# Grouped-query attention: reciprocal softmax sums spread over partitions through a row in DRAM instead of by products with the identity

## The reference, cut to what matters

```
q, k = rms_norm(q, q_norm_w), rms_norm(k, k_norm_w)
q, k = apply_rope(q, cos, sin), apply_rope(k, cos, sin)
p = softmax(einsum("bhgqd,bhkd->bhgqk", q, k) * 64 ** -0.5)
o = einsum("bhgqk,bhkd->bhgqd", p, v)
return o @ w_o
```

## Time and profile before

| what | value |
| --- | --- |
| time, median of 3 runs | 3609.38 us (3599.21 to 3609.42) |
| time of the profiled execution | 3618.67 us |
| span of the profiled execution, first to last instruction | 3616.9 us |
| TensorE busy | 3342.2 us, 92% of the span |
| VectorE busy | 1868.7 us, 52% |
| ScalarE busy | 1185.8 us, 33% |
| GpSimd busy | 942.6 us, 26% |
| mean granted TensorE clock | 0.964 of full |
| DMA, mean over the span | 64 GB/s |

### The profile page before, as it was taken

One profiled execution on the slowest core, in us unless ns is written; L12 is line 12 of the kernel. 1 busy time (PEld: TensorE's weight loads), 2 busy tenths in 40 slices (PEclk: granted clock), 3 DMA queues, 4 the chain that ended last, 5 costly groups with the idle time before them and its releaser, 6 DMA issues. The chain is left out here.

```text
span 3616.9 us, 51583 instructions
## 1 busy us (share of the span) xinstructions
PE 3342.2 (92%) x20797; PEld 3084.3 (85%) x20797; DVE 1868.7 (52%) x2655; ACT 1185.8 (33%) x2106; POOL 942.6 (26%) x726
## 2 busy tenths in 40 slices
PE   5898898998889999999988999999798999999997
PEld 4777777887789999999988777777598999999996
DVE  4555555555155554555545555565416545555454
ACT  3334344444232222122223555555413121222111
POOL 1122112222233322223233121221133322332221
PEclk8999999998899999999999999999899999999998
DMA  6333343113211111111112111101231111111101
GB/s 240 108 107 113 112 125 116 51 40 121 87 42 47 41 53 35 41 37 39 54 38 78 38 30 26 35 23 35 97 99 58 42 36 41 41 37 56 35 29 59
DMA packets 206659, 229.78 MB, mean 64 GB/s; under 512 B 30564, under 2 KB 173533, under 8 KB 205341
## 3 DMA queue, kind: packets, MB, share of 16 engines
q1 hardware_dynamic: 186973, 162.69, 14.8%
q10 hardware_dynamic: 11664, 42.47, 3.5%
q0 software_dynamic: 7856, 22.29, 1.7%
HBM read 181.79 MB, written 31.98 MB: 59 GB/s over the span
## 5 line engine op out<-in xcount | busy, mean ns | idle before, releaser
L205 PE MATMUL psum<-Hh,wh 128*128 128x384 f32 x3360 | 1142.2, 340 | 52.6 <-ACT Hh L377 14.7
L206 PE MATMUL psum<-Hh,wl 128*128 128x384 f32 x3360 | 1131.0, 337 | 0.0
L207 PE MATMUL psum<-Hl,wh 128*128 128x384 f32 x3360 | 1130.9, 337 | 0.0
L286 DVE SCALAR_TENSOR_TENSOR x<-psum,mod,x 128x384 f32<-128x384 f32 (+2 forms) x768 | 377.4, 514 | 684.6 <-PE psum L207 643.2
L205 PEld LDWEIGHTS psum<-Hh,wh 128*128 128x128 f32 x3360 | 636.6, 189 | 63.3 <-issue 35.5
L206 PEld LDWEIGHTS psum<-Hh,wl 128*128 128x128 f32 x3360 | 636.8, 190 | 0.0
L207 PEld LDWEIGHTS psum<-Hl,wh 128*128 128x128 f32 x3360 | 636.5, 189 | 0.0
L816 POOL TENSOR_TENSOR wl<-wr,wh 128x1024 fp32r<-128x1024 f32 x88 | 219.8, 2498 | 986.6 <-ACT wh L735 986.6
L766 ACT ACTIVATE ff_u<-psum 128x768 f32<-128x768 f32 x88 | 71.6, 814 | 1109.2 <-PE psum L207 1109.2
L205 PE MATMUL psum<-ff_ah,ff_dh 128*128 128x384 f32 x1056 | 365.1, 346 | 29.4 <-POOL ff_al L838 20.7
L964 DVE SCALAR_TENSOR_TENSOR ff_c<-ff_u,par,ff_c 128x1153 f32<-128x1153 f32 x176 | 377.4, 2144 | 15.8 <-DVE ff_c L961 5.2
(11 more groups left out here) (217 smaller groups left out, 4267.8 us busy)
## 6 DMA issues: line engine op xcount, KB each, us to landing
wr<-w_up SPq DMA_DIRECT2D x88, 512.0 KB, 3.9
ff_dr<-w_down SPq DMA_DIRECT2D x22, 1024.0 KB, 6.1
da_mw<-mod_w ACTq DMA_DIRECT2D x40, 512.0 KB, 3.9
wr<-mod_w ACTq DMA_DIRECT2D x40, 512.0 KB, 4.8
wr<-w_qkv_diff SPq DMA_DIRECT2D x24, 512.0 KB, 19.2
x<-x_save SPq DMA_DIRECT2D x16, 576.0 KB, 7.5
in_mw<-mod_w SPq DMA_DIRECT2D x8, 1024.0 KB, 12.2
Hh<-oh_save SPq DMA_DIRECT2D x14, 576.0 KB, 9.8
```

The lines of the kernel that those rows point to most:

```text
L205: pe.matmul(out, w_hi, m_hi, start=start, stop=False)
L206: pe.matmul(out, w_lo, m_hi, start=False, stop=False)
L207: return pe.matmul(out, w_hi, m_lo, start=False, stop=stop)
L286: last = dve.scalar_tensor_tensor(g.x[:, m, lo:hi], g.PS[:, bank, lo - n * NB:hi - n * NB], g.mod[:, gate + m, cond:cond + 1], g.x[:, m, l ...
```

## The change

For each pair, the reciprocals no longer go through TensorE. DVE writes `rl` with the two heads outermost. SP's new `spread_sums` waits for them, sends them to a small row buffer in DRAM (`rl_rows`, 512 numbers of 4 bytes, one by one), waits for that to land, and reads them back with two DMAs, each of which puts one head's row of up to 256 numbers on 64 partitions of `rb`. ACT copies half a bank, DVE multiplies `yb` by `rb`. The division of pair 4 moves from step 0 of the next head (where it stood behind nothing but its wait) to step 1, behind that step's maxima. In SP's program the swap of head j+1 comes behind `spread_sums(j, 0)`; `spread_sums(j, 1)` to `(j, 4)` come behind the swap and ahead of the next head's weight load; the first output weights come between `spread_sums(7, 0)` and `(7, 1)`; and the wait for head 6's stores and `load_outputs`, unchanged in the text, now stand behind `spread_sums(7, 4)`. TensorE's first wait for the reciprocals goes; each third block of the value product also waits for the copy of head m = 0's group.

```
--- before.py
+++ after.py
@@ -152,6 +152,7 @@
         g.lam = sb("lam", [P, 4])
         g.Hh = sb("Hh", [P, KC, T], F32R)
         g.Hl = sb("Hl", [P, KC, T], F32R)
+        g.rl_rows = nc.dram_tensor("rl_rows", [2, 2, 2, P], F32, kind="Internal").ap()
         g.x_save = nc.dram_tensor("x_save", [P, KC, T], F32, kind="Internal").ap()
         g.wr = sb("wr", [P, 2, KC, P])
         g.wh = sb("wh", [P, 2, KC, P], F32R)
@@ -1832,17 +1833,13 @@
         "cos": ([P, NS], F32), "sin": ([P, NS], F32), "q": ([P, T], F32), "rot": ([P, NS], F32), "sq": ([P, T], F32),
         "nqh": ([P, 2, T], F32R), "nql": ([P, 2, T], F32R), "nkh": ([P, 2, KW], F32R), "nkl": ([P, 2, KW], F32R),
         "v": ([P, 2, KW // P, P], F32), "e": ([P, 2, NKEY], F32), "pt": ([P, 2, TT, 2 * P], F32),
-        "yb": ([P, 2, 2 * P], F32), "y": ([P, 2, 2 * P], F32), "yh": ([P, 2 * P], F32R), "yl": ([P, 2 * P], F32R),
+        "yb": ([P, 2 * P], F32), "rb": ([P, 2, 2 * P], F32), "y": ([P, 2, 2 * P], F32), "yh": ([P, 2 * P], F32R), "yl": ([P, 2 * P], F32R),
         "nm": ([P, 2], F32), "nb": ([P, 2], F32), "l": ([P, 4, 2], F32), "rl": ([P, 2, 2], F32), "wq": ([P, 1], F32),
         "ms": ([P, TT, 2], F32), "rk": ([P, 2, TT, 2], F32), "r": ([P, 2, TT, 2], F32)},
         "tab w_in0 w_in1 w_hi w_lo free0 free1 full free2 free3 free4 ahead side sq_d ck_in ck_d cv_in ko_d v_st k_st ms_d r_d normed kswap swap rope"
-        " s_mm mx nmax exp rl_d pv_out y_d y_split y_out wq_d wo_in0 wo_in1 wo_hi wo_lo o_in")
+        " s_mm mx nmax exp rl_d rl_out rl_in pv_out y_d y_split y_out wq_d wo_in0 wo_in1 wo_hi wo_lo o_in")
     free = {"F": b.free0, "C": b.free1, 0: b.free2, 1: b.free3, 2: b.free4}
     w_in = [b.w_in0, b.w_in1]
-    BC0 = 2 * P
-
-
-
     early = b.pt[:, :, :, :].rearrange("p m c q -> p (m c q)")
     k = [early[:, p * KW:(p + 1) * KW] for p in range(2)]
     vt = [early[:, 2 * KW:2 * KW + T], early[:, 0:T]]
@@ -1906,6 +1903,22 @@
                 ring.wait_read(sp, free, ("vt", p, 2))
                 for m in range(2):
                     sp.dma_start(a.new_v_gqa[0, 0, 2 * p + m], b.v[:, p, KW // P - 1, m * DH:(m + 1) * DH]).then_inc(b.v_st, 16)
+
+            def spread_sums(j, p):
+
+                n, done = PAIRS[p][1], len(PAIRS) * j + p
+                sp.wait_ge(b.rl_d, done + 1)
+                if done >= 2:
+                    sp.wait_ge(b.rl_in, 32 * (done - 1))
+                rows = g.rl_rows[done % 2]
+                sp.dma_start(rows.rearrange("m i q -> q (m i)"), b.rl[:, :, :].rearrange("p m i -> p (m i)"),
+                             allow_slow_non_contiguous=True).then_inc(b.rl_out, 16)
+                if done >= 2:
+                    sp.wait_ge(b.y_d, done - 1)
+                sp.wait_ge(b.rl_out, 16 * done + 16)
+                for m in range(2):
+                    sp.dma_start(b.rb[m * DH:(m + 1) * DH, done % 2, 0:n * P],
+                                 rows[m, 0:n].rearrange("i q -> (i q)").partition_broadcast(DH)).then_inc(b.rl_in, 16)
 
             load_w(("K", 1))
             load_w(("V", 0))
@@ -1930,11 +1943,15 @@
             for j in range(HEADS):
                 if j + 3 < HEADS:
                     load_w(("Q", j + 3))
+                spread_sums(j, 0)
                 if j + 1 < HEADS:
                     swap_queries(j + 1)
-            sp.wait_ge(b.w_lo, len(UNITS) - 2)
-            sp.wait_ge(b.full, ring.done(("Q", HEADS - 1, NN - 1)))
-            first_out_weights(g, sp, b, 1)
+                for p in range(1, len(PAIRS)):
+                    if (j, p) == (HEADS - 1, 1):
+                        sp.wait_ge(b.w_lo, len(UNITS) - 2)
+                        sp.wait_ge(b.full, ring.done(("Q", HEADS - 1, NN - 1)))
+                        first_out_weights(g, sp, b, 1)
+                    spread_sums(j, p)
             sp.wait_ge(b.y_out, 32 * len(PAIRS) * (HEADS - 1) + 16)
             load_outputs(g, sp, b)
             sp.wait_ge(b.o_in, OUT_LOADS)
@@ -2013,8 +2030,7 @@
                     act.wait_ge(b.full, ring.done(use))
                     if done:
                         act.wait_ge(b.y_d, done)
-                    act.activation(b.yb[:, :, 0:n], ring.bank(g, use).rearrange("p (a t) -> p a t", a=2)[:, :, 0:n],
-                                   ACT.Copy).then_inc(free[ring.place[use]], 1)
+                    act.activation(b.yb[:, 0:n], ring.bank(g, use)[:, 0:n], ACT.Copy).then_inc(free[ring.place[use]], 1)
 
             act.wait_ge(b.wq_d, 1)
             for n in range(2):
@@ -2185,16 +2201,12 @@
                 use, (t0, n) = ("PV", j, p), PAIRS[p]
                 out = ring.bank(g, use)
                 ring.wait_free(pe, free, use)
-                pe.wait_ge(b.rl_d, len(PAIRS) * j + p + 1)
-                for i in range(n):
-                    broadcast_heads(g, pe, out[:, BC0 + i * P:BC0 + (i + 1) * P], b.rl[:, i, :])
                 if p == 0 and j % 4 == 0:
                     pe.wait_ge(b.cv_in, 16 * 4)
                 t, nk = t0 + n - 1, keys(t0) // P
                 for c in range(nk):
-                    if nk == 1:
-                        ring.wait_read(pe, free, ("T", j, t, 0, 0))
                     if c % 3 == 0:
+                        ring.wait_read(pe, free, ("T", j, t, 0, c // 3))
                         ring.wait_read(pe, free, ("T", j, t, 1, c // 3))
                     for m in range(2):
                         last = pe.matmul(out[m * DH:(m + 1) * DH, 0:n * P], b.v[:, j // 4, value_chunk(t0, c), m * DH:(m + 1) * DH],
@@ -2299,14 +2311,17 @@
             def sums(j, p):
                 t0, n = PAIRS[p]
                 dve.wait_ge(b.exp, 2 * (TILES * j + t0 + n))
-                dve.reciprocal(b.rl[:, 0:n, :], b.l[:, t0 % 4:t0 % 4 + n, :]).then_inc(b.rl_d, 1)
+                if j or p:
+                    dve.wait_ge(b.rl_out, 16 * (len(PAIRS) * j + p))
+                dve.reciprocal(b.rl[:, :, 0:n], b.l[:, t0 % 4:t0 % 4 + n, :].rearrange("p i m -> p m i")).then_inc(b.rl_d, 1)
 
             def divide(j, p):
                 n, done = PAIRS[p][1] * P, len(PAIRS) * j + p
                 ring.wait_read(dve, free, ("PV", j, p))
+                dve.wait_ge(b.rl_in, 32 * (done + 1))
                 if done >= 2:
                     dve.wait_ge(b.y_split, 2 * (done - 1))
-                dve.tensor_tensor(b.y[:, done % 2, 0:n], b.yb[:, 0, 0:n], b.yb[:, 1, 0:n], ALU.mult).then_inc(b.y_d, 1)
+                dve.tensor_tensor(b.y[:, done % 2, 0:n], b.yb[:, 0:n], b.rb[:, done % 2, 0:n], ALU.mult).then_inc(b.y_d, 1)
 
             dve.tensor_scalar(b.wq[:, :], g.par[:, PC_QN:PC_QN + 1], SCALE, None, ALU.mult).then_inc(b.wq_d, 1)
             dve.wait_ge(b.tab, 16)
@@ -2347,8 +2362,10 @@
                         maxima(j, s)
                     if s == TILES and j + 1 < HEADS:
                         maxima(j + 1, 0)
+                    if s == 1 and j:
+                        divide(j - 1, len(PAIRS) - 1)
                     for use in gqa_previous(j, s):
-                        if use[0] == "PV":
+                        if use[0] == "PV" and s:
                             divide(*use[1:])
                     if j + 1 < HEADS and s in ROPE_AT:
                         rope(("Q", j + 1), ROPE_AT[s])
```

## The result

The changed kernel takes 3705.16 us (median of 4 runs, 3702.07 to 3706.89) against 3606.07 us before: a ratio of 1.0276 (95% interval 1.0257 to 1.0295), 99 us slower. Forecast were 3616.8 us, reckoned from the first three runs before (3609.38; with a fourth the median is 3606.07), and no measurable change. The profiled execution spans 3705.1 us.

What follows compares the result with a forecast made beforehand. TensorE, busy 184.7 of 200 us in the GQA stage, was taken to bound the kernel. Terms: -15.9 + 0.3 + 23.0 = +7.4 us on 3609.4, giving 3616.8 us; forecast's own range 3612 to 3621, overall 3604 to 3628.

Steps and rivals of the forecast that it cites:

- Term 1: GQA heads: broadcast products leave TensorE, which is earlier by 15.9 us together; bounds 12 and 21.9.
- Term 2: Inside the heads: the way through DRAM takes about 5.5 us from the reciprocal, bounds 4.9 and 9, and costs nothing.
- The prediction's own sign of being wrong: TensorE's wait for DVE's copies growing by many us, meaning that the sums are late, would show the prediction wrong.
- the 13 us that I gave the other pairs: Pairs other than 1: 13 us or more between reciprocal and division to cover the way through DRAM.
- the 8.4 us of pair 1: Tightest pair: 8.4 us are there after the swap for store and loads, against 5.5 needed.
- Taken: 0: Heads: the way through DRAM, covered by about 8 us between reciprocal and division, was priced at no loss.
- The rival that DVE stands for the sums: Heads: store and loads need 9.9 us, pair 1 is 1.5 us late in seven heads, +10 us, 3627; chance 0.10.
- Term 3: Head 7: first output weights come later, ACT is 0.9 us late, half of it free; cost 0.3 us, bounds 0 and 3.
- Term 4: Stage end: the outputs' reload falls behind the last `spread_sums`, exposed, net 23.0 us; bounds 18.6 and 25.
- my lower bound of 18.6: Stage end: the exposed reload's cost in us if the barrier took the 1.9 us seen where another stage begins.

Runs made afterwards that it cites:

- no_way: Changed kernel without the calls of `spread_sums` and every wait for it, DVE multiplying by a cosine table row: 3589.96 us, ratio 0.9967 to before.
- unwaited: Changed kernel with all its DMAs and SP's waits, but the store sends a constant and DVE waits for none of it: 3630.1 us, ratio 1.0063 to before.
- own_line: Changed kernel with the 512 4-byte pieces stored 64 bytes apart, loads reading the cosine table: 3614.9 us, ratio 1.0039 to before.
- weights_early: Changed kernel with only the first output weights issued in head 6 instead of head 7: 3696.6 us, ratio 1.0239 to before.
- reload_early: Changed kernel with only the reload of the outputs issued in head 7 ahead of the way of pair 1: 3666.7 us, ratio 1.0180 to before.
- experiment 6: The run reload_early: changed kernel with only the outputs' reload moved ahead of the way of pair 1 in head 7; 3666.7 us.
- pieces16: Changed kernel with the store writing the same 512 numbers as 128 contiguous pieces of 16 bytes: 3611.1 us, ratio 1.0011 to before.
- sbuf_store: Changed kernel with the 512 4-byte pieces stored into a dead SBUF tile, loads reading the cosine table: 3613.8 us, ratio 1.0025 to before.
- pieces8: Changed kernel, complete, with the store writing 256 pieces of 8 bytes and the reload still behind the last pair: 3614.75 us, ratio 1.0036 to before.
- pieces8_early: pieces8 with the outputs' reload issued in head 7 ahead of the way of pair 1: 3603.7 us, ratio 0.9999 to before.
- best: Changed kernel with 8-byte pieces, reload in POOL's queue, output weights in head 6, last pair by identity products as before: 3590.9 us, ratio 0.9964 to before.
- gap8: Changed kernel with the 512 4-byte pieces stored 8 bytes apart, loads reading the cosine table: 3628.8 us, one execution.
- shift8: gap8 with the whole buffer moved by 32 bytes: 3617.1 us, one execution.

## Why the prediction was wrong, step by step

- **Term 1, products off TensorE: right.** 15.9 us forecast, 14.7 us measured by no_way.
- **Term 2, the way through DRAM: the step that failed.** "I take 2.5 us out ... bounds 4.9 and, with 4.5 out and 3.8 back, 9." The store took 10.1 us. The loads, 3.3 us in the median, were as bounded. The prediction's own sign of being wrong came true: TensorE's wait for DVE's copies grew from 5.4 to 38.3 us. With 10.1 + 0.5 + 3.3 = 14 us the way is longer than the 13 us that I gave the other pairs, not only than the 8.4 us of pair 1. "Taken: 0" was 70 us (changed kernel against unwaited, heads 0 to 6), of which 51 are waits of TensorE and 19 its slower products; the prediction priced no loss of clock from a late DVE. I costed the store from rows of whole transfers and by the number of its pieces; none of those rows had small pieces side by side in DRAM, so the row bounded the wrong quantity. The rival that DVE stands for the sums named the mechanism and its consequence for the copies, but its price was 10 us and its chance 0.10, both set by the same rows.
- **What the page says.** Of the Trainium skill's "DMA: Bandwidth & Descriptors" I named the rule on one descriptor per element; own_line has one descriptor per element too and takes 2.0 us, so this rule alone isn't what bit. The same page of the Trainium skill says in its "Anatomy" section, of DMAs on GpSimd's path, that the fixed price is mostly the receipt of the write. These are SP's; the silent 9 us behind the last packet fit that it was the receipt that grew, but no run separates it.
- **Term 3, the output weights: sign right, size wrong.** 0.3 us forecast, bounds 0 and 3; 8.6 us by weights_early, 11.4 in head 7's stretch. It was 0.9 us late by my reckoning with a store of 2.5; the store at this place took 11.0, and 0.9 + 8.5 = 9.4 us is near the 9.1 that ACT stood. The same error counted twice.
- **Term 4, the reload: exposed as said.** 23.0 us forecast with 2.5 us of store, 27.4 measured with the slow one (11.1 us at this place). With a short store the end is 26.4 to 28.2 us against 9.4, so 17 to 19 us more: nearer to my lower bound of 18.6. From the first reload issue (2687.90) to the next stage (2711.41) are 23.5 us, near the 22.2 forecast for the transfer, whose packets run until about 2710.4. So the barrier costs about 1 us there and not 6.3. Reload_early gives back 15 us at the end.
- **The sum** by the measured terms: -14.7 + 70 + 11 + 27 = 93 us, against 99. The rest is within what the unexplained spread of the heads between builds (22.7 us in experiment 6) leaves open. The kernels with a short store and the late reload were 6 to 12 us slower than before (pieces16, sbuf_store, own_line, pieces8), close to the +7.4 forecast. That is partly luck: there the end costs 17 to 19 us and not 23, and the heads keep part of the loss.

## What to carry to other kernels

Before a wait is put behind a small DMA store, look at what its pieces share in DRAM: the same 512 words cost 2 us or 10 by their spacing alone, and whoever waits in line behind them pays it again at each place. When a step joins an in-order queue, list what now stands behind it (here the reload and the output weights) and cost the step's upper bound through each of them, not its likely value. Price a stand that reaches TensorE above its idle time: here 70 us for 51. Bound an unseen operation by its form, not by the size of the nearest transfer; where no row has that form, the range has to say so.

## What the runs showed of the hardware that was not expected

- The landing of a store of small pieces to DRAM depends on how many lie within 64 bytes: 2.0 us at 1, 3.4 to 3.9 at 8, 10.1 at 16, while 256 or 512 pieces at the same spacing gave 3.8 and 3.9. Contiguous pieces of 16 bytes (4 in 64 bytes) took 1.6 us, and the store into SBUF 2.1. The packets themselves are through in half a microsecond. Why it climbs so steeply from 8 to 16, and whether 64 bytes is the right stretch to count in, wasn't settled; 16 in 64 bytes was run with one layout only.
- A 2 KB store behind 8.3 MB of loads of the same queue took 14.8 us to be confirmed instead of 3.4 (pieces8_early); with the loads in another queue and still running it took 9.2 (best), issued later in the reload.
- TensorE's products in heads 0 to 6 took 496.1 us at a mean granted clock of 0.89 where DVE made it wait, and 477.2 us at 0.93 where it didn't (unwaited). Two single executions with the same 3.9 us from store to loads differed the same way: gap8 529 us for these heads, 484.5 busy at 0.91, and shift8 515 us, 473.4 busy at 0.94.
- Two builds with the same program in heads 0 to 6 differed by 22.7 us there, with the slow store in both (the changed kernel and reload_early); the runs of each of the two agree within 5 us. Why is open.
